# First shift's columns of blocks two to four on VectorE, conditions spread into the input tiles' buffer, parameters loaded with the third and fourth block

## The chip, the cores and the metric

The kernel runs on one core of a Trainium2 chip. The metric is the device time of one execution in microseconds, as the median of several runs; lower is better. The engines of the core are TensorE (PE, with its weight loads as PEld), VectorE (DVE), ScalarE (ACT), GpSimd (POOL) and SyncE (SP, which here only issues transfers). GpSimd issues transfers too, on a queue of its own.

## The reference, cut to what matters

One layer of a diffusion trunk: three tiles of 128 tokens (one prompt tile, two sample tiles) of width 2048, attention of three kinds, and a mixture of experts. Ahead of both halves stands a modulation whose vectors come from a condition; the prompt tile has the condition `c_ctx`, the two sample tiles have `c`:

```python
def modulate(h, shift, scale):
    return h * (1 + scale) + shift

def adaln(cond, w_mod, b_mod):
    m = jax.nn.silu(cond) @ w_mod + b_mod
    return jnp.split(m[:, None, :], 6, axis=-1)

sh1, sc1, g1, sh2, sc2, g2 = adaln(cond_ctx, lp["w_mod"], lp["b_mod"])
mix, ctx_t = context_mixer(modulate(rms_norm(xp, lp["g_attn"]), sh1, sc1), lp)
```

`w_mod` is 2048 x 12288 in fp32, so each of its six groups is 16 MB. The change is about the first two groups, the first shift (SH1) and the first scale (SC1), which are needed before any projection can start. All is fp32.

## The kernel before, in words

**Weights.** SyncE loads all weights in a fixed order of units of up to 1 MB into a ring of 12 slots (`units` in `plan`, the loop at line 776). Unit m waits until unit m - 12 is done with its slot (`frees`, lines 674 to 717). Two of the nine column chunks of the input projection, `ckv` (320 columns) and `cq0` (384 columns), are "early": they are computed while the modulation vectors are still being made. Their weights are cut into four pieces along the rows and go into two buffers of their own (`early_w`, lines 784 to 788); piece i waits until piece i - 2 has been used.

**The first blocks.** The 2048 columns of SC1 and SH1 are cut into four blocks of 512 columns (i = 0 to 3, called blocks one to four). A block has eight units, four of SC1 and then four of SH1, each with 512 rows of the weight; behind them come the two early weights of the block. On TensorE `first_unit` (line 842) multiplies a unit by the two conditions and a gain row (`csil`, three columns), four products side by side. When the four units of a group are in, VectorE adds the bias row (`first_copy`, L1626), TensorE turns the row into columns (`first_turn`, L859), and VectorE takes the columns out of the bank (`first_mod`, L1636, L1637, L1633). The outcome is `mod_t`: per row k of the transposed input one scale and one shift for each condition, with 128 features on the partitions. Then VectorE scales the transposed input in place (`hmod`, L1645), row by row, and TensorE multiplies the rows by the early weights (`early_part`, L883).

**The order on TensorE** is written out by hand (`next_units`, line 905, and the loop at line 912). A block of early projections has eight parts (four rows, two chunks each). After part 0 come units 0 and 1 of the *next* block, after part 1 units 2 and 3, then one unit after each of the parts 2 to 5; the scale row is turned after part 3 and the shift row after part 6. The first block's units stand before the loop, between the transposes of the input (`turn_xn`, L871). A block starts once both of its early weights have landed (line 879) and its first row is scaled (line 881).

```python
for n in ((0, 1), (2, 3), (4,), (5,), (6,), (7,), (), ())[part]:
    first_unit(i, n // 4, n % 4)
if part in (3, 6):
    first_turn(i, part // 6)
```

**GpSimd** loads the bias rows and the gain row at the start (lines 2143 to 2145), then works out the norms of the input (lines 2147 to 2150), then waits for turns: at the third (line 2151) it loads the rest of the constants, at the seventh (line 2153, the fourth block's scale) the gains and biases of all norms (lines 2154 to 2158) and the cached keys (lines 2159 to 2162). The norm of the first projection waits for these (line 1823).

**ScalarE** takes half of the transposed input out of its banks (line 1398) and then has nothing to do until the first projection is complete (L1431).

**After the blocks** the other projections, the attentions, the later four modulation groups, the output projection and the experts follow. The last modulation group is summed on VectorE (`g2_step`, L1800): a row of its weight, times the condition's value in that row, is added to a sum; two passes over 128 x 2048 per row.

Of the kernel before, what the change touches and what calls it, by code (L numbers as in the profile page):

```python
# [24 lines left out]
P = 128  # L25
D = 2048
# [48 lines left out]
FIRST_GROUPS = (SC1, SH1)  # L75
OUT_ORDER = [(0, 0), (0, 1), (0, 2), (1, 0), (1, 1), (1, 2), (2, 0), (2, 1), (3, 0), (3, 1), (2, 2), (3, 2)]
# [74 lines left out]
def plan():  # L151
# [27 lines left out]
    for i in range(4):  # L179
        units.extend(("first", g, i, m) for g in FIRST_GROUPS for m in range(4))  # L180
# [130 lines left out]
def by_units(w_mod, w_in, w_o):  # L311

    out = {}
    first = w_mod[0].reshape(P, 4, 4, 6, 4, 512)[:, :, :, list(FIRST_GROUPS)]
    out["w_first"] = first.transpose(3, 4, 1, 0, 2, 5).reshape(2, 4, 4, P, D)
# [7 lines left out]
def build(nc, ins, outs):  # L323
# [54 lines left out]
    with ExitStack() as ctx:  # L378
# [73 lines left out]
        junk_x, first_rows = r3_at(0, D), (r3_at(9728, D), r3_at(D, D))  # L452
# [108 lines left out]
        def acc_done(n):  # L561
# [43 lines left out]
        cols_in, brow_full, brow_ready, bias_full, bias_ready, wr_scaled = (sem(n) for n in (  # L605
            "cols_in", "brow_full", "brow_ready", "bias_full", "bias_ready", "wr_scaled"))
# [4 lines left out]
        ge_in, ge_out, re_in, re_out = sem("ge_in"), sem("ge_out"), sem("re_in"), sem("re_out")  # L611
# [22 lines left out]
        def unit_source(u, e=0):  # L634
# [5 lines left out]
            if kind == "first":  # L640
                _, g, i, m = u
                return ins["w_first"][FIRST_GROUPS.index(g), i, m].rearrange("p (q n) -> p q n", q=4), (4, 512)
# [32 lines left out]
        for i in range(4):  # L675
            for m in range(4):
                for c, g in enumerate(FIRST_GROUPS):
                    u = unit_no[("first", g, i, m)]
                    if m == 3:
                        frees[u] = (first_full, 2 * i + c + 1)  # L680
                    else:
                        slot_uses[ring_slot(u)] += 1
        uses = [0] * SLOTS
        for u in range(unit_no[("first", FIRST_GROUPS[1], 3, 3)] + 1):
# [87 lines left out]
        def _(sp):  # L772
# [3 lines left out]
            for m, u in enumerate(units):  # L776
# [5 lines left out]
                if u[0:2] == ("first", FIRST_GROUPS[1]) and u[3] == 3:  # L782
                    i = u[2]
# [53 lines left out]
        def _(pe):  # L837
# [4 lines left out]
            def first_unit(i, c, m):  # L842
# [4 lines left out]
                if m == 0:  # L847
                    if i:
                        pe.wait_ge(modt_ready, 2 * i + c - 1)
# [5 lines left out]
            def first_turn(i, c):  # L855

                pe.wait_ge(first_copied, 2 * i + c + 1)
# [3 lines left out]
                mm.then_inc(modt_full, 1)  # L861

# [70 lines left out]
            def tp_bank(s):  # L933
# [3 lines left out]
                else:  # L937
                    pe.wait_ge(modt_ready, 8)
# [40 lines left out]
            def spread_row():  # L979
# [5 lines left out]
                mm.then_inc(bias_full, 1)  # L985
# [389 lines left out]
        def _(act_e):  # L1375
# [24 lines left out]

            def cols_out(n):
# [171 lines left out]
            e.activation(g_s, g_s, ACT.Exp).then_inc(ge_out, 1)  # L1573
# [24 lines left out]
        def _(v):  # L1598
# [8 lines left out]
            v.memset(csil[:, :, 2:3], 0.0)  # L1607
            v.memset(first_ps[0][:, :], 0.0)
# [13 lines left out]
            def first_copy(i, c):  # L1622
                if i == 0 and c == 0:
                    v.wait_ge(first_rows_in, 3 * 16)
                v.wait_ge(first_full, 2 * i + c + 1)
# [3 lines left out]
            def first_mod(i, c):  # L1629
                v.wait_ge(modt_full, 2 * i + c + 1)  # L1630
# [10 lines left out]
            def hmod(i):  # L1641
                v.wait_ge(modt_ready, 2 * i + 2)
                for k in range(4 * i, 4 * i + 4):
# [3 lines left out]
                    last.then_inc(h_ready, 1)  # L1647

# [10 lines left out]
            v.wait_ge(xn_read_a, 6)  # L1659
            v.wait_ge(xn_read_v, 6)  # L1660
# [626 lines left out]
```

## Time and profile before

| What | Value |
| --- | --- |
| Median of 3 runs | 1689.63 us (1689.2 to 1691.83) |
| Profiled execution | 1689.92 us, of which the span is 1688.1 us |
| TensorE busy | 1587.0 us (94%) |
| VectorE, ScalarE, GpSimd busy | 690.1, 263.6, 106.1 us |
| Moved by the transfers | 581.94 MB, mean 345 GB/s |
| Chain that ended last | TensorE 67%, transfers 18%, VectorE 4% of the span |

The span is the profile's; the run's own time is 1.8 us longer. The window view gives the busy time of each engine in a stretch, the granted clock of TensorE (1.00 is 2.4 GHz, 0.50 is 1.2 GHz), the busy share of the transfer engines and their rate. In the timeline, instructions of one form that follow each other are merged into one row; a product in fp32 leaves two records. In the view of one line, "DMA to landing" is the time from the issue of a transfer to its landing.

### The profile page before, as it was taken

The page shows a single profiled execution, that of the slowest core. Times are in us where ns is not written, and L with a number is a line of the kernel's source. Part 1 is how long each engine was busy: PE and PEld are TensorE (multiplying, and loading weights), DVE is VectorE, ACT ScalarE, POOL GpSimd, SP SyncE. Part 2 cuts the span into 40 slices and gives each one's busy share as a digit, 9 for nine tenths or more (in the row PEclk, how much of TensorE's full clock was granted, in tenths as well). Part 3 has the DMA queues.
Part 4 walks back from the last instruction along what each step waited for, and adds up shares of the span by engine and source line. Part 5 has one row for each costly group of instructions (what it writes and reads, how often), then busy time and mean ns, then how long its engine had stood idle before and what let it go on. Part 6 is the DMA issues. An engine that isn't in the chain of part 4 may idle for free.

```text
span 1688.1 us, 18209 instructions
## 1 busy us (share of the span) xinstructions
PE 1587.0 (94%) x6671; PEld 654.3 (39%) x6716; DVE 690.1 (41%) x1361; ACT 263.6 (16%) x706; POOL 106.1 (6%) x192
## 2 busy tenths in 40 slices
PE   5999999999999999999999899899999899988998
PEld 2455555544434444443332332333233233233322
DVE  2113132113245893443444335444434434544444
ACT  2004221112133000011101101110110111011010
POOL 1022100100020100000000000000000000000000
PEclk8999999999999999999999999999999999999999
DMA  9993643535199765599999999999999999999995
GB/s 394 420 384 124 231 193 108 223 112 217 53 369 410 275 264 247 202 363 426 425 428 427 429 428 427 427 428 429 426 425 426 427 427 423 428 426 428 421 428 240
DMA packets 60526, 581.94 MB, mean 345 GB/s; under 512 B 9129, under 2 KB 10121, under 8 KB 16105
## 3 DMA queue, kind: packets, MB, share of 16 engines
q1 hardware_dynamic: 53120, 557.34, 79.8%
q0 software_dynamic: 6064, 23.22, 3.6%
q10 hardware_dynamic: 1296, 0.77, 0.2%
q8 instruction: 28, 0.46, 0.1%
q14 instruction: 18, 0.15, 0.0%
HBM read 584.06 MB, written 7.05 MB: 350 GB/s over the span
## 4 chain that ended last, share of the span: by engine, by line
PE 67%; DMA 18%; DVE 4%; issue 2%; ACT 1%; SPq 0%; POOL 0%; ACTq 0%
PE bank L1304 23%; DMA ring<-in_w 17%; PE bank L1052 13%; PE bank L1031 7%; PE bank L1214 7%; PE bank L1337 3%; DVE r L1800 2%; PE bank L926 2%; PE bank L1139 2%; PE bank L1263 2%; PE bank L1200 1%; PE bank L1114 1%; PE bank L1122 1%; PE bank L1319 1%; PE bank L1071 1%
## 5 line engine op out<-in xcount | busy, mean ns | idle before, releaser
L1304 PE MATMUL bank<-ring,r 128*64 128x512 f32 x1920 | 466.6, 616 | 45.1 <-DMA ring<-in_w 44.9
L1304 PEld LDWEIGHTS bank<-ring,r 128*64 128x64 f32 x1920 | 129.1, 139 | 300.6 <-issue 300.6
L1052 PE MATMUL bank<-ring,r 128*128 128x384 f32 (+1 forms) x672 | 240.7, 517 | 0.0
L2020 DVE TENSOR_TENSOR bank<-bank,r 128x512 f32<-128x512 f32 x180 | 126.0, 700 | 262.8 <-PE bank L1214 262.8
L1337 PE MATMUL bank<-ring,mod_row 128*64 128x512 f32 x896 | 195.6, 594 | 8.0 <-ACT mod_row L1553 7.9
L1031 PE MATMUL bank<-ring,r 128*128 128x512 f32 x384 | 170.0, 595 | 0.0
L1052 PEld LDWEIGHTS bank<-ring,r 128*128 128x128 f32 x672 | 126.3, 190 | 102.7 <-issue 43.2
L1214 PE MATMUL bank<-r 128*128 128x512 bf16 x495 | 137.7, 382 | 7.1 <-issue 7.0
L2022 DVE TENSOR_TENSOR r<-r,bank 128x512 f32<-128x512 f32 x180 | 123.8, 688 | 6.2
L1337 PEld LDWEIGHTS bank<-ring,mod_row 128*64 128x64 f32 x896 | 75.2, 137 | 118.7 <-issue 108.5
L1214 PEld LDWEIGHTS bank<-r 128*128 128x128 bf16 x540 | 38.0, 97 | 167.4 <-DVE r L2022 97.4
L1031 PEld LDWEIGHTS bank<-ring,r 128*128 128x128 f32 x384 | 71.2, 191 | 79.4 <-issue 79.3
L2043 DVE TENSOR_SCALAR gains<-bank,w_now 128x512 f32<-128x512 f32 x30 | 22.5, 751 | 175.0 <-PE bank L1337 162.0
L1800 DVE SCALAR_TENSOR_TENSOR r<-ring,csil,r 128x2048 f32<-128x2048 f32 x32 | 74.3, 2348 | 5.6 <-DMA r<-in_b_mod 5.0
L1828 DVE SCALAR_TENSOR_TENSOR r<-r,small,gains 128x128 f32<-128x128 f32 (+1 forms) x91 | 27.2, 343 | 120.9 <-POOL small L2138 115.8
L1876 DVE TENSOR_REDUCE small<-bank 128x1 f32<-128x384 f32 (+1 forms) x48 | 22.5, 468 | 129.7 <-PE bank L1114 77.3
L1431 ACT ACTIVATE r<-bank 128x128 f32<-128x128 f32 (+2 forms) x79 | 22.1, 289 | 324.6 <-PE bank L1052 215.8
L883 PE MATMUL bank<-r 128*128 128x320 f32 (+1 forms) x192 | 64.2, 481 | 1.2 <-DVE r L1645 1.2
L1542 ACT ACTIVATE r<-bank 128x512 f32<-128x512 f32 x30 | 17.8, 595 | 301.7 <-PE bank L1200 301.7
L1548 ACT ACTIVATE gain_row<-bank 128x512 f32<-128x512 f32 x16 | 9.6, 597 | 275.3 <-PE bank L1304 261.6
L2266 POOL COPY gat_now<-r 128x1 int32 x14 | 2.5, 182 | 747.9 <-PE bank L1200 747.9
L926 PE MATMUL bank<-ring,csil 128*2 128x512 f32 x384 | 47.4, 592 | 0.0
(283 smaller groups left out, 1237.8 us busy)
## 6 DMA issues: line engine op xcount, KB each, us to landing
ring<-in_w SPq DMA_DIRECT2D x180, 2048.0 KB, 17.4
ring<-in_w_mod SPq DMA_DIRECT2D x64, 1024.0 KB, 11.7
ring<-in_w_first SPq DMA_DIRECT2D x32, 1024.0 KB, 25.8
ring<-in_w SPq DMA_DIRECT2D x18, 1024.0 KB, 9.3
ring<-in_w_o SPq DMA_DIRECT2D x16, 1024.0 KB, 6.6
r<-mod_d POOLq DMA_DIRECT2D x8, 1024.0 KB, 8.4
ring<-in_w_aq SPq DMA_DIRECT2D x8, 768.0 KB, 11.3
ring<-in_w_bq SPq DMA_DIRECT2D x8, 768.0 KB, 12.9
```

The source lines that it names most:

```text
L883: mm = pe.matmul(early_bank[3 * c + t][:, 0:w], h_t[:, k, t * P:(t + 1) * P], early_w[c][i % 2][:, jj, :], start=(k == 0), stop=(k == KD - 1))
L926: mm = pe.matmul(mod_ps[32 * q:32 * q + 2, :], csil[:, k, 0:2], ring[:, ring_slot(m), q * 512:(q + 1) * 512], start=(k == 0), stop=(k == K ...
L1031: mm = pe.matmul(acc[acc_of(a)][:, :], qo[:, t, k, :], wu[:, j, :], start=(k == 0), stop=(k == KD - 1))
L1052: mm = pe.matmul(acc[acc_of(a)][:, 0:w], h_t[:, k, t * P:(t + 1) * P], wu[:, j, :], start=(k == 0), stop=(k == KD - 1))
L1139: mm = pe.matmul(out, v, prob_t[u % 2][:, i, :] if g == "C" else prob_ab[batch_of(u) % 2][:, i, :], start=(i == 0), stop=(i == len(tiles) ...
L1214: mm = pe.matmul(y_ps[k % 4][:, :], of_token[:, t * P:(t + 1) * P], y_part[:, n_part, c, :], start=(n_part == 0), stop=(n_part == 2))
L1263: mm = pe.matmul(ps[64 * c:64 * c + 64, :], xg_t[:, j, 64 * c:64 * c + 64], first_place(u)[:, j % 4 * 512:j % 4 * 512 + 512], start=(j == ...
L1304: mm = pe.matmul(ps[64 * c:64 * c + 64, :], xg_t[:, j, 64 * c:64 * c + 64], big_cut(slot_of(u), (8, 512))[:, j % 8, :], start=(j == 0), st ...
L1337: mm = pe.matmul(y_ps[c][64 * h:64 * h + 64, :], act_t[:, f, 64 * h:64 * h + 64], big_cut(slot_of(u), (2, D))[:, f % 2, c * 512:(c + 1) * ...
L1800: last = v.scalar_tensor_tensor(out=g2_sum[:, c, :], in0=ring[:, ring_slot(m), :], scalar=csil[:, k, c:c + 1], in1=g2_sum[:, c, :], op0=AL ...
L2020: v.tensor_tensor(ps[:, :], ps[:, :], g2b[:, min(t, 1), cols], ALU.mult).then_inc(strip_scaled, 1)
L2022: return v.tensor_tensor(x1[:, t, cols], x1[:, t, cols], ps[:, :], ALU.add)
```

## The change

Blocks two to four of SH1 no longer go through TensorE. Their 12 columns of `mod_t` (128 features each, k = 4 to 15) become units of a new kind, `("shift", k)`: the transposed weight, 128 output features on the partitions and 2048 inputs along the row, 1 MB each, in the place of the four SH1 units of the block. VectorE multiplies such a unit by a condition that is spread over all partitions, and sums along the row, one pass for each condition (`shift_columns`).

The conditions are spread at the start: GpSimd loads them as rows, TensorE multiplies them by a column of ones into banks (`spread_cond`, eight products, placed after the second and the third of the first block's shift units), and ScalarE takes them out with a Silu into the part of the input tiles' buffer that is free after the transposes (`cond_all`). TensorE waits for all eight before block one.

ScalarE scales the transposed input for k = 4 to 15; VectorE keeps k = 0 to 3. On TensorE one unit of the next block's scale stands after each of the parts 1 to 4 of a block, and its turn after part 5. GpSimd loads the gains and biases at the turn of the third block's scale, the cached keys at that of the fourth's. Two semaphores of the later stages are shared with the new steps, to stay within their number (not shown). The core of the diff:

```diff
     for i in range(4):
-        units.extend(("first", g, i, m) for g in FIRST_GROUPS for m in range(4))
+        units.extend(("first", SC1, i, m) for m in range(4))
+        units.extend(("shift", 4 * i + m) if i else ("first", SH1, i, m) for m in range(4))
...
+    out["w_shift"] = w_mod[0][:, SH1 * D + SHIFT_FROM * P:(SH1 + 1) * D].T.reshape(KD - SHIFT_FROM, P, D)
+    out["b_shift"] = b_mod[0][SH1 * D:(SH1 + 1) * D].reshape(KD, P).T
...
-        junk_x, first_rows = r3_at(0, D), (r3_at(9728, D), r3_at(D, D))
+        junk_x, first_rows = r3_at(0, D), (r3_at(9728, D), r3_at(D, 512))
+        ones_c, cond_rows, b_shift = r3_at(D + 512, P), r3_at(D + 640, 2, 512), r3_at(D + 1664, KD)
+        cond_all, junk_s = r2[:, 0:2 * D].rearrange("p (c n) -> p c n", c=2), r2[:, 2 * D:2 * D + D // 2].bitcast(BF16)
...
+                    if c and i:
+                        frees[unit_no[("shift", 4 * i + m)]] = (modt_ready, shift_count(4 * i + m))
+                        continue
...
+            def spread_cond(n0, n1):
+                for n in range(n0, n1):
+                    c, q = n // 4, n % 4
+                    mm = pe.matmul(spread_bank[n][:, :], ones_c[32 * q:32 * q + 1, :], cond_rows[32 * q:32 * q + 1, c, :],
+                                   start=True, stop=True)
+                mm.then_inc(spread_full, 1)
...
-            for m in range(4):
-                first_unit(0, 1, m)
+            first_unit(0, 1, 0)
+            first_unit(0, 1, 1)
+            pe.wait_ge(first_rows_in, 6 * 16)
+            pe.wait_ge(xn_read_a, 6)
+            pe.wait_ge(xn_read_v, 6)
+            spread_cond(0, 4)
+            first_unit(0, 1, 2)
+            pe.wait_ge(modt_ready, scale_count(0))
+            pe.wait_ge(cond_ready, 1)
+            spread_cond(4, 8)
+            first_unit(0, 1, 3)
             first_turn(0, 1)
+            pe.wait_ge(cond_ready, 8)
             def next_units(i, part):
-                for n in ((0, 1), (2, 3), (4,), (5,), (6,), (7,), (), ())[part]:
-                    first_unit(i, n // 4, n % 4)
-                if part in (3, 6):
-                    first_turn(i, part // 6)
+                if 1 <= part <= 4:
+                    first_unit(i, 0, part - 1)
+                elif part == 5:
+                    first_turn(i, 0)
...
+            for n in range(8):
+                c, q = n // 4, n % 4
+                ps = (xn_banks + (first_ps[0], xn_banks[0]))[n]
+                e.wait_ge(spread_full, 1 + c)
+                e.activation(cond_all[:, c, q * 512:(q + 1) * 512], ps[:, :], ACT.Silu).then_inc(cond_ready, 1)
+            for k in range(SHIFT_FROM, KD):
+                e.wait_ge(modt_ready, column_count(k))
+                for c, cols in enumerate((slice(0, P), slice(P, T))):
+                    last = e.activation(h_t[:, k, cols], h_t[:, k, cols], ACT.Identity, bias=mod_t[:, 1, k, c:c + 1],
+                                        scale=mod_t[:, 0, k, c:c + 1])
+                last.then_inc(h_ready, 1)
...
+            def shift_columns(k):
+                m = unit_no[("shift", k)]
+                v.wait_ge(*full_of(m))
+                if k == SHIFT_FROM:
+                    v.wait_ge(cond_ready, 8)
+                else:
+                    v.wait_ge(modt_ready, shift_count(k - 1))
+                w = ring[:, ring_slot(m), :]
+                for c in range(2):
+                    last = v.tensor_tensor_reduce(junk_s, w, cond_all[:, c, :], 1.0, b_shift[:, k:k + 1], ALU.mult, ALU.add,
+                                                  mod_t[:, 1, k, c:c + 1])
+                    if c == 0:
+                        after(last)
+                last.then_inc(modt_ready, 1)
...
-            hmod(0)
+            first_hmod()
             for i in range(1, 4):
-                for c in range(2):
-                    first_copy(i, c)
-                    first_mod(i, c)
-                hmod(i)
+                first_copy(i, 0)
+                shift_columns(4 * i)
+                first_mod(i, 0)
+                for k in range(4 * i + 1, 4 * i + 4):
+                    shift_columns(k)
...
+            g.dma_start(b_shift, ins["b_shift"]).then_inc(first_rows_in, 16)
+            g.dma_start(cond_rows[0:P:32, 0, :], ins["c_ctx"].rearrange("(q n) -> q n", q=4)).then_inc(first_rows_in, 16)
+            g.dma_start(cond_rows[0:P:32, 1, :], ins["c"][0].rearrange("(q n) -> q n", q=4)).then_inc(first_rows_in, 16)
...
-            g.wait_ge(modt_full, 7)
+            g.wait_ge(modt_full, first_count(2, 0))
             for name, dst in gain_of.items():
                 g.dma_start(dst, ins[name][0].partition_broadcast(P)).then_inc(gains_in, 16)
...
+            g.wait_ge(modt_full, first_count(3, 0))
             g.dma_start(cached["c"], ins["cache_c_kv"][0, 0]).then_inc(cache_k_in, 16)
...
-            g.wait_ge(modt_full, 8)
             load_row(LATER_GROUPS[0])
```

`first_count(2, 0)` is 4 and `first_count(3, 0)` is 5: with the shift turns of blocks two to four gone, these are the turns of the third and the fourth block's scale.

## Rows read from the trace of the kernel before

**Rows 1.** The page: TensorE and the transfers in 40 slices of the span.
```profile
PE   5999999999999999999999899899999899988998
...
DMA  9993643535199765599999999999999999999995
```

**Rows 2.** Windows of 20 us: stretch, length, busy us per engine, PEclk, DMA, GB/s.
```profile
80.00:100.00 20.00, 20.00 (x105) 8.93 (x104) 3.96 (x11) 0.00 (x0) 0.00 (x0) 1.00 1.01 420
...
140.00:160.00 20.00, 18.73 (x64) 10.41 (x63) 5.99 (x26) 8.99 (x45) 5.71 (x12) 1.00 0.01 5
```

**Rows 3.** Timeline, 37 to 130 us: start, length, engine, line, operation, tiles, records.
```profile
38.16 3.54 PE L883 MATMUL bank<-r 128*128 128x320 f32 x6 [1.16 <-DVE r L1645]
...
62.82 3.80 PE L883 MATMUL bank<-r 128*128 128x384 f32 x12
...
70.94 0.11 PEld L851 LDWEIGHTS bank<-ring,csil 128*3 128x3 f32 x4 [0.32 <-DMA ring<-in_w_first]
...
72.33 1.88 PE L883 MATMUL bank<-r 128*128 128x320 f32 x6
...
74.15 1.04 PE L851 MATMUL bank<-ring,csil 128*3 128x512 f32 x8
...
87.53 3.80 PE L883 MATMUL bank<-r 128*128 128x384 f32 x12
...
112.24 16.38 PE L883 MATMUL bank<-r 128*128 128x384 f32 x54
```

**Rows 4.** Early weights (L788), one issue each: blocks three and four, then landing.
```profile
L788 SPq DMA_DIRECT2D r<-in_w_cq x1: 327/327/327, 65.0 to 65.0; - x1
...
DMA to landing us min/median/max: 19.1/19.1/19.1
...
L788 SPq DMA_DIRECT2D r<-in_w_cq x1: 327/327/327, 89.7 to 89.7; - x1
...
DMA to landing us min/median/max: 17.7/17.7/17.7
```

**Rows 5.** VectorE passes over 128x2048, two sources and one: ns min/median/max, first and last start.
```profile
L1800 DVE SCALAR_TENSOR_TENSOR r<-ring,csil,r x32: 2341/2351/2352, 557.4 to 639.3; 128x2048 f32<-128x2048 f32 x32
...
L1613 DVE TENSOR_SCALAR r<-r,small x3: 1276/1285/1286, 9.3 to 18.3; 128x2048 f32<-128x2048 f32 x3
```

**Rows 6.** Ring loads (L781) of block four: issues 68.9 to 73.2 and 75.4 to 77.6.
```profile
L781 SPq DMA_DIRECT2D ring<-in_w_first x3: 2126/2133/2138, 68.9 to 73.2; - x3
...
DMA to landing us min/median/max: 25.2/25.5/25.8
...
L781 SPq DMA_DIRECT2D ring<-in_w_first x2: 433/1284/2134, 75.4 to 77.6; - x2
...
DMA to landing us min/median/max: 26.1/26.3/26.4
```

**Rows 7.** ScalarE's groups to 150 us: busy us, mean ns, then idle before and releasers.
```profile
L1398 ACT ACTIVATE r<-bank 128x512 f32<-128x512 f32 x6 | 3.4, 592 | 1.9 <-PE bank L871 1.9
...
L1431 ACT ACTIVATE r<-bank 128x128 f32<-128x128 f32 (+2 forms) x15 | 4.6, 316 | 115.2 <-PE bank L883 103.4 <-PE bank L1052 9.6 <-PE bank L1071 2.0
```

**Rows 8.** GpSimd's timeline; the bracket is the idle time before, with its releaser.
```profile
8.38 0.19 POOL L2149 TENSOR_SCALAR small<-small 128x1 f32<-128x1 f32 x1 [2.06 <-ACT r L1387]
...
104.29 0.55 POOL L2155 DMA_DIRECT2D gains<-in_a_qn  x1 [48.79 <-PE bank L859]
```

**Rows 9.** Ring loads (L781) that follow block four's early weights.
```profile
L781 SPq DMA_DIRECT2D ring<-in_w_cq x4: 430/449/2124, 90.1 to 91.6; - x4
...
DMA to landing us min/median/max: 20.4/25.6/29.6
```

**Rows 10.** Queues, 104 to 125 us: packets, MB, share of the 16 engines.
```profile
q0 software_dynamic: 608, 1.05, 23.2%
```

**Rows 11.** Windows of 1 us, columns as in rows 2: TensorE's clock falls and returns.
```profile
31.00:32.00 1.00, 0.00 (x1) 0.00 (x0) 0.00 (x0) 0.00 (x0) 0.00 (x0) 0.93 1.01 410
32.00:33.00 1.00, 0.57 (x4) 0.11 (x8) 0.00 (x0) 0.00 (x0) 0.00 (x0) 0.50 1.05 431
...
42.00:43.00 1.00, 1.00 (x12) 0.19 (x8) 0.00 (x0) 0.00 (x0) 0.00 (x0) 0.95 1.04 434
```

More of the change, by code:

```diff
@@ L75, with first_count, shift_count, scale_count @@
 FIRST_GROUPS = (SC1, SH1)
+SHIFT_FROM = 4
+def first_count(i, c):
+    return i + 2 if i else c + 1
+def shift_count(k):
+    i, j = k // 4, k % 4
+    return 2 + 5 * (i - 1) + (j + 2 if j else 1)
+def scale_count(i):
+    return 2 + 5 * (i - 1) + 2 if i else 1
+def column_count(k):
+    return max(shift_count(k), scale_count(k // 4)) if k >= SHIFT_FROM else 2
 OUT_ORDER = [(0, 0), (0, 1), (0, 2), (1, 0), (1, 1), (1, 2), (2, 0), (2, 1), (3, 0), (3, 1), (2, 2), (3, 2)]
@@ L308, with by_units @@
         ("state_c_kv", (1, 1, P, KV_RANK)), ("state_c_krope", (1, 1, P, ROPE))]
-def by_units(w_mod, w_in, w_o):
+def by_units(w_mod, b_mod, w_in, w_o):
     out = {}
-    first = w_mod[0].reshape(P, 4, 4, 6, 4, 512)[:, :, :, list(FIRST_GROUPS)]
-    out["w_first"] = first.transpose(3, 4, 1, 0, 2, 5).reshape(2, 4, 4, P, D)
+    first = w_mod[0].reshape(P, 4, 4, 6, 4, 512)
+    out["w_scale"] = first[:, :, :, SC1].transpose(3, 1, 0, 2, 4).reshape(4, 4, P, D)
+    out["w_shift0"] = first[:, :, :, SH1, 0].transpose(1, 0, 2, 3).reshape(4, P, D)
+    out["w_shift"] = w_mod[0][:, SH1 * D + SHIFT_FROM * P:(SH1 + 1) * D].T.reshape(KD - SHIFT_FROM, P, D)
+    out["b_shift"] = b_mod[0][SH1 * D:(SH1 + 1) * D].reshape(KD, P).T
     rows = w_in[0].reshape(4, 4, P, -1)
@@ L641, in unit_source @@
                 _, g, i, m = u
[L642 removed]
+                w = ins["w_scale"][i, m] if g == SC1 else ins["w_shift0"][m]
+                return w.rearrange("p (q n) -> p q n", q=4), (4, 512)
+            if kind == "shift":
+                return ins["w_shift"][u[1] - SHIFT_FROM], (D,)
             if kind == "in":
@@ L683, in build @@
         uses = [0] * SLOTS
-        for u in range(unit_no[("first", FIRST_GROUPS[1], 3, 3)] + 1):
+        for u in range(unit_no[("shift", KD - 1)] + 1):
             if u not in frees:
@@ L781, in _ @@
                 sp.dma_start(cut(slot, shape), src).then_inc(slot_full[slot], 16)
-                if u[0:2] == ("first", FIRST_GROUPS[1]) and u[3] == 3:
-                    i = u[2]
+                if u == ("first", SH1, 0, 3) or u[0] == "shift" and u[1] % 4 == 3:
+                    i = u[1] // 4 if u[0] == "shift" else 0
                     for c, name in enumerate(EARLY):
@@ L1639, in first_mod, with first_hmod @@
                                            op0=ALU.add, op1=ALU.mult).then_inc(modt_ready, 1)
-            def hmod(i):
-                v.wait_ge(modt_ready, 2 * i + 2)
-                for k in range(4 * i, 4 * i + 4):
+            def first_hmod():
+                v.wait_ge(xn_read_a, 6)
+                v.wait_ge(xn_read_v, 6)
+                v.wait_ge(modt_ready, column_count(0))
+                for k in range(SHIFT_FROM):
                     for c, cols in enumerate((slice(0, P), slice(P, T))):
@@ L2277 @@
     arrays = {f"in_{n}": np.ascontiguousarray(inputs[n]) for n in IN_NAMES if n not in ("w_in", "w_o")}
-    for n, a in by_units(inputs["w_mod"], inputs["w_in"], inputs["w_o"]).items():
+    for n, a in by_units(inputs["w_mod"], inputs["b_mod"], inputs["w_in"], inputs["w_o"]).items():
         arrays[f"in_{n}"] = np.ascontiguousarray(a)
```

37 lines of the change are left out of this document (20 added, 17 removed).

## The prediction

> **What bounds the kernel now.** I read the page first, then the stretch before the first projections, then the transfers there. Over the whole span TensorE has nearly no idle slice, so what shortens or lengthens its work early moves the end by as much [rows 1]. In the first 100 us the DMA engines are full as well, at 420 GB/s; only from 140 us, with every ring slot filled, do they rest [rows 2]. So this stage has two limits side by side, and the change touches both.
>
> The timeline shows TensorE's side. The merged rows that begin with the last piece of a block start at 62.82, 87.53 and 112.24 us: 24.7 us a block [rows 3]. Between the pieces of the early projections (1.88 us with 320 columns) stand the units of the first shift and scale (1.04 us) [rows 3]. The last block has no units: 54 records in 16.38 us, 48 of them its own, so 14.3 us for a block of projections alone; block four starts at 114.3 and ends at 128.6 us.
>
> The transfers' side: a block needs eight units and two early weights, 9.83 MB, or 23.4 us at 420 GB/s. The last early weight of block three was issued at 65.03 and landed 19.1 us later, at 84.1; that of block four at 89.75 + 17.7 = 107.45 us [rows 4]. The distance is 23.4 us, as by the bytes. TensorE began block four only 6.9 us after its last weight was there. **That lead is all that faster engines can win here**: no byte of the weights goes away.
>
> **The change, part by part.**
>
> *Units taken off TensorE.* A block loses four units and one turn of ten such pieces; (24.7 - 14.3) / 10 = 1.04 us each, so 5.2 us a block and 15.6 us over three. TensorE's block becomes 19.5 us, shorter than the transfers' 23.4. From block two on TensorE then waits for data, and of the 15.6 us at most 6.9 can be kept.
>
> *Columns on VectorE.* Twelve columns, two passes each over 128x2048 of two fp32 sources in SBUF. The trace has no such pass. Nearest is the two-source pass of the last modulation group, which reads the ring too: 2.35 us; below lies the one-source pass of that size, 1.28 us, above it twice the two-source pass, 4.7 us, should the sum cost a second reading [rows 5]. I take 2.35, same shape and number of sources. A column is 4.7 us, a block 18.8 plus a copy and a modulation of about 1.1: 19.9, within 23.4. The order on VectorE matters: a block's first column stands behind the copy of its scale row, which waits for TensorE's fourth unit. In block two that copy ends near 54 us (block one starts at 38.16, four pieces and four units in, the first at the low clock), and the twelve columns could be through at 54 + 24 x 2.35 + 3 = 113 us. Block four's columns also wait for their data: today the fourth scale unit lands at 68.9 + 25.2 = 94.1, the next unit near 96.9, the last at 77.6 + 26.4 = 104.0 us [rows 6]. With the delay below, the first column starts near 101 and the fourth ends near 120 us; ScalarE's scaling adds 0.7, and TensorE wants it at about 123. So the columns hide, with 2 to 3 us to spare.
>
> The Trainium skill, Vector Engine (DVE) Microarchitecture Reference, section on points that are easy to get wrong, says that an STT-shaped instruction with two SBUF sources that are not bf16 runs at half rate, for want of a port for the accumulator. The existing pass has that shape and those sources and shows no half rate (2.35 us beside 1.28 with one source); with an accumulator no run here shows it. By that rule of the Trainium skill a column would be 9.4 us, my estimate, twice the measured pass.
>
> *Scaling on ScalarE.* Twelve pairs, by the 316 ns mean of its early activations some 0.7 us a pair [rows 7]; it has sat idle for over 100 us here, so they cost the first 0.7 us of a column's delay, counted above. VectorE sheds as much.
>
> *The spread.* Eight one-row products and eight Silu of some 592 ns (the copies of that size [rows 7]) go in before block one, and TensorE waits for all eight. Four such products take 1.04 us if they share the array like a unit's four [rows 3], and 3.5 us if one by one (0.30 us a record by the last row of [rows 3], scaled to 512 columns, two records each); double at the low clock. Most fits into the waits for units up to 32 us; the delay of block one is 0 to 7 us. It costs nothing, because block two would be over near 80 us and must wait for the weights of block three at 84 and later. If that wait were gone, it would cost those 0 to 7.
>
> *GpSimd's queue.* Three more loads stand ahead of its first scaling, at 0.55 us an issue [rows 8], 1.65 in all; it idles 2.06 us there [rows 8]. Nothing.
>
> *SyncE.* As many transfers in the same order; but a ring slot of a shift column is now freed by VectorE. The unit that lands at 94.1 reuses the slot of the fourth column of block two, free near 74 us: 20 us ahead, and other transfers are queued before it. Nothing, until a pass exceeds some 3 us.
>
> *The parameters.* Now they are asked for at 104.29 us [rows 8], when the last early weights are about to land, and what they push back is the next weights. Those four units, issued up to 91.6, should follow at 107.45 + 7.5 (3.15 MB) = 114.95 and landed at 91.6 + 29.6 = 121.2: 6.25 us late [rows 9]. Beside them the software queue took 23.2% of the engines' time over 21 us, 4.9 us, for 1.05 MB [rows 10]. After the change the gains and biases (597 KB) go out at the third block's scale turn, near 76 us (its last unit landed at 70.9 [rows 3]), and the cached keys (416 KB) at the fourth's, near 103: **ahead of the early weights on which block four waits.** By bytes the first lot is 59%, 3.7 us, all in front; of the other 2.55 us I take half; the new small loads 0.2. Bounds: 0.2, if the packets slip behind, and 6.5. I take 5.2, since two thirds are asked for 30 us before the deadline.
>
> *The clock.* TensorE fell to half its clock at 32 us, after it had waited for units, and was back at 42 us, four us into block one; its first piece there took 3.54 us instead of 1.88 [rows 3, 11]. That row prices a cold start at 1.7 us for the piece and about 1.9 for the block. With the change TensorE stands still for some 6 us before block four (block three over near 107, weights at 112.7). Bounds 0 and 1.9; I take 1.0, since no wait of this length after a busy stretch is in the trace.
>
> **Sum.** Block four starts at 107.45 + 5.2 = 112.65 instead of 114.3, and ends at 112.65 + 14.3 + 1.0 = 127.95 instead of 128.6: 0.7 us earlier. Behind it the first projection has its weights 6 us before it needs them, and the work up to the expert stage follows TensorE, so the end moves by as much. The profiled execution took 1689.92 us (span 1688.1), 0.3 above the median: 1689.2 for it, 1688.9 us as a median. Bounds of the forecast: a delay of 6.5 and a cold start, 114.0 + 14.3 + 1.9 = 130.2 (+1.6), and a delay of 3.5 and none, 111 + 14.3 = 125.3 (-3.3); that is 1686.3 to 1691.2.
>
> **Rivals.**
>
> *The parameters don't hold up the weights* (faster). If GpSimd issues them slowly or the engines favour the hardware queue, block four starts at 107.65 and ends at 122.0, or 123.9 with a cold start: 4.7 to 6.6 us saved, 1683.0 to 1684.9. For it: issues on GpSimd will stand beside two-source VectorE passes, which this trace has not; slowed issues would land later, perhaps too late to matter. Against it: today's 6.25 us push, on the same queues. (The Trainium skill, GPSIMD Engine Reference, section Specifications, says that GpSimd shares its SBUF interfaces with VectorE and contends with its instructions that have two SBUF inputs; no run here shows by how much.)
>
> *The pass with a sum is slow* (slower). The columns set the end when 54 + 24x + 3 + 4.3 exceeds 128.6, from x = 2.8 us a pass. At 4.7 the chain ends at 174 us, 45 later: 1735. Against it: the existing pass. For it: an instruction the trace doesn't show. It is what the rule quoted above from the Trainium skill's Vector Engine (DVE) Microarchitecture Reference would do; the trace does not bear it out without an accumulator, and is silent with one.
>
> *The change doesn't do what it says*: no, the units and the turn are gone from TensorE's list.
>
> **Chances.** Forecast, with the clock and the parameters within their bounds, 0.63; parameters out of the way 0.24; slow pass 0.10; another delay before block one than I can place 0.03. A measurement tells about 0.2%, 3.4 us: below 1686.2 counts as faster, above 1693.0 as slower. That gives 0.24 faster, 0.63 within, 0.13 slower. The range takes in the forecast and most of the first rival, 1683.5 to 1692.0; the likeliest case alone is 1686.3 to 1691.2.
>
> **What would show it.** Right: TensorE waits for early weights before blocks three and four; block four starts within 2 us of 112.7 and runs 14 to 16; the parameter loads land before its weights; the passes take 2.35 us and VectorE rests before each block's first. Wrong: block four starts by 109 (parameters cheap), passes over 2.8 us with TensorE waiting for ScalarE's h, or a start of block one so late that block two ends after 88.

## The result, and the profile of the changed kernel

The changed kernel takes 1693.72 us (median of 10 runs, 1691.29 to 1696.04), beside 1689.3 us for the kernel before in the same comparison (10 runs). The ratio is 1.0022, 95% interval 1.0014 to 1.003: slower by 0.2%, 3.7 us by the ratio and 4.4 as the difference of the medians. The forecast, 0.7 us the other way, and its range up to 1692.0 both missed.

The profiled execution is the fastest of the ten, 1691.29 us with a span of 1689.5 (before 1688.1). TensorE's busy time fell by 8.2 us (1578.8 against 1587.0): units and turns alone fell by 15.9 us (12.6 and 3.3, forecast 15.6), but the spread added 2.3 and the blocks' products, in part at the low clock, 3.2. VectorE's rose to 736.0. So the work was moved as meant, and the time went into waits. TensorE's timeline from the end of block two on:

```profile
75.73 3.80 PE L929 MATMUL bank<-r 128*128 128x320 f32 x12
90.14 6.66 PE L929 MATMUL bank<-r 128*128 128x320 f32 x12 [10.62 <-DMA r<-in_w_cq]
...
109.22 3.80 PE L929 MATMUL bank<-r 128*128 128x320 f32 x12
114.17 7.57 PE L929 MATMUL bank<-r 128*128 128x320 f32 x24 [1.15 <-DMA r<-in_w_cq]
122.82 3.82 PE L929 MATMUL bank<-r 128*128 128x320 f32 x12 [1.08 <-ACT r L1468]
127.72 3.82 PE L929 MATMUL bank<-r 128*128 128x320 f32 x12 [1.08 <-ACT r L1468]
...
131.75 4.68 PE L1108 MATMUL bank<-ring,r 128*128 128x384 f32 x14
```

Block three waits 10.62 us for its early weights and starts at 90.14, no earlier than in the kernel before, where it follows on the piece that begins at 87.53 [rows 3]: all that TensorE won in block two is lost here. Block four starts at 114.17, as before, but then its rows wait for ScalarE (L1468), and the next projection (L1108) starts at 131.75, 2.9 us later than before (L1052 there):

```profile
128.85 1.46 PE L1052 MATMUL bank<-ring,r 128*128 128x384 f32 x4
```

The transfers show why block three waits. The `cq0` weights of block three and of block four were issued at 59.19 and 88.71 us; they landed 30.9 and 25.4 us later, at 90.1 and 114.1:

```profile
L824 SPq DMA_DIRECT2D r<-in_w_cq x1: 327/327/327, 59.2 to 59.2; - x1
...
DMA to landing us min/median/max: 30.9/30.9/30.9
...
L824 SPq DMA_DIRECT2D r<-in_w_cq x1: 2749/2749/2749, 88.7 to 88.7; - x1
...
DMA to landing us min/median/max: 25.4/25.4/25.4
```

Between them GpSimd issued the gains, from 76.17 to 81.57 us. Windows of the same trace (stretch, length, busy us of PE, PEld, DVE, ACT, POOL, then granted clock, DMA share, GB/s):

```profile
72.00:78.00 6.00, 6.00 (x30) 3.68 (x28) 5.73 (x6) 0.99 (x2) 1.83 (x4) 1.00 1.02 426
78.00:82.00 4.00, 1.53 (x5) 0.57 (x3) 3.93 (x7) 0.98 (x2) 3.57 (x7) 1.00 1.18 330
82.00:86.00 4.00, 0.00 (x0) 0.00 (x0) 3.82 (x5) 0.98 (x2) 0.00 (x0) 0.53 0.80 134
86.00:90.00 4.00, 0.00 (x0) 0.00 (x0) 3.85 (x3) 0.98 (x2) 0.00 (x0) 0.50 1.00 342
90.00:96.00 6.00, 5.86 (x11) 3.54 (x12) 3.12 (x4) 0.98 (x2) 0.00 (x0) 0.51 1.01 409
```

From 82 to 86 us the transfer engines are 80% busy and move 134 GB/s, a third of the usual rate. Both queues are slow then (packets, MB, share of the 16 engines): the gains take 37.2% for 0.14 MB, and the weights beside them 42.9% for 0.40 MB.

```profile
q1 hardware_dynamic: 74, 0.40, 42.9%
q0 software_dynamic: 64, 0.14, 37.2%
```

TensorE stands still meanwhile, its clock falls to 0.50 (1.2 GHz, called cold below), and the first 12 records of block three take 6.66 us instead of 3.80.

On VectorE the new work is as cheap as hoped. The pass with its sum, the read of the accumulator and ScalarE's scaling:

```profile
L1733 DVE CUSTOM_DVE_ANT_0 r<-ring,r x24: 2341/2351/2352, 53.3 to 124.3; 128x2048 bf16<-128x2048 f32 x24
L1733 DVE DVE_READ_ACCUMULATOR2_ANT mod_t<- x24: 80/82/84, 55.5 to 126.6; 128x1 f32 x24
...
L1468 ACT ACTIVATE r<-r,mod_t x24: 492/539/587, 58.4 to 127.1; 128x128 f32<-128x128 f32 x12, 128x256 f32<-128x256 f32 x12
```

### The profile page after: what moved, and what is told of

Read it like the earlier page. It is cut to its first block, busy times and chain, and to the rows that moved or that the text cites. A ratio compares the mean times of both kernels' runs of the same rounds, so it can differ in the third digit from the quotient of the medians.

```text
span 1689.5 us, 18067 instructions
## 1 busy us (share of the span) xinstructions
PE 1578.8 (93%) x6567; PEld 653.2 (39%) x6612; DVE 736.0 (44%) x1380; ACT 279.6 (17%) x738; POOL 106.4 (6%) x195
## 4 chain that ended last, share of the span: by engine, by line
PE 68%; DMA 16%; DVE 4%; issue 2%; ACT 1%; SPq 0%; POOL 0%; ACTq 0%
PE bank L1360 24%; DMA ring<-in_w 15%; PE bank L1108 13%; PE bank L1270 7%; PE bank L1087 7%; PE bank L1393 3%; DVE r L1889 2%; PE bank L982 2%; PE bank L1195 2%; PE bank L1319 2%; PE bank L1256 1%; PE bank L1408 1%; PE bank L1342 1%; PE bank L1170 1%; PE bank L1178 1%
## 5 line engine op out<-in xcount | busy, mean ns | idle before, releaser
L1108 PE MATMUL bank<-ring,r 128*128 128x384 f32 (+1 forms) x672 | 240.7, 517 | 0.0
L1108 PEld LDWEIGHTS bank<-ring,r 128*128 128x128 f32 x672 | 126.2, 190 | 102.8 <-issue 43.2
L1733 DVE CUSTOM_DVE_ANT_0 r<-ring,r 128x2048 bf16<-128x2048 f32 x24 | 56.4, 2350 | 1.3
L929 PEld LDWEIGHTS bank<-r 128*128 128x128 f32 x192 | 37.4, 204 | 46.8 <-issue 14.5
```

Of the source, the lines that this page charges most:

```text
L929: mm = pe.matmul(early_bank[3 * c + t][:, 0:w], h_t[:, k, t * P:(t + 1) * P], early_w[c][i % 2][:, jj, :], start=(k == 0), stop=(k == KD - 1))
L1108: mm = pe.matmul(acc[acc_of(a)][:, 0:w], h_t[:, k, t * P:(t + 1) * P], wu[:, j, :], start=(k == 0), stop=(k == KD - 1))
L1733: last = v.tensor_tensor_reduce(junk_s, w, cond_all[:, c, :], 1.0, b_shift[:, k:k + 1], ALU.mult, ALU.add, mod_t[:, 1, k, c:c + 1])
```

## Experiments

Four terms were in question: the place of the parameter loads, what makes them dear, the columns' chain, and the cold clock. Medians and ratios are over several runs; rows and starts come from one profiled execution of each kernel, and two traces of the changed kernel differ by 1.0 us at the next projection (part 5).

### 1. Where the parameters are asked for

**The fourth block's turn** (e1): `- g.wait_ge(modt_full, first_count(2, 0))`, `+ g.wait_ge(modt_full, first_count(3, 0))` ahead of the gains, all else as changed.

> The changed kernel with the gains and biases asked for at the fourth block's scale turn, as before the change. Theory P (the parameter loads stall the weights, TensorE waits and comes back at half clock, and the scale copy and the columns behind it come late): block three starts near 84.5 us instead of 90.1, without a long wait; the same push, some 6 us, now falls on the weights of block four, which starts near 113 and ends at 128 to 130 instead of 131.5. 1690 to 1692 us. Theory C (the columns on VectorE set the end by themselves): block four still ends near 131, 1693.7 us.

**After block four's early weights** (e5): `- g.wait_ge(modt_full, first_count(2, 0))`, `+ g.wait_ge(early_in[1], 2 * 32)`.

> The changed kernel with all parameter loads behind the landing of the last early weight. Theory P: no push on any early weight; block three starts near 84.5, block four near 108, its columns are ready at about 102 to 118, it ends at 122 to 124; 1682.5 to 1685 us. Theory C: the end of block four moves by less than 2 us, 1692 to 1694 us. If the norm behind the first projections then waits for the gains, up to 4 us of this come back.

**The kernel before, with the gains moved alone** (e3): `- g.wait_ge(modt_full, 7)`, `+ g.wait_ge(modt_full, 5)` ahead of the gains; the cached keys stay at 7.

> The kernel before with one part of the change alone: gains and biases asked for at the third block's scale turn, the cached keys left at the fourth's. Theory P: the weights of block three land near 90 and those of block four near 113.5 instead of 84.1 and 107.45; TensorE, which starts these blocks at 89.6 and 114.3 there, loses at most 1 us: 1689 to 1690.5 us. If the loads pushed by only 3.7 us, as forecast, there is no change at all: 1689.3 us.

| Kernel | Median us (runs) | Ratio to before (95%) | Next projection starts (one trace) |
| --- | --- | --- | --- |
| before, for e1, e5 and e3 | 1690.09 (27) | | 128.85 |
| changed | 1693.72 (10) | 1.0022 (1.0014 to 1.003) | 131.75 |
| e1, gains at the fourth | 1688.62 (11) | 0.999 (0.9981 to 0.9999) | 127.71 |
| e5, all after early weights | 1686.58 (11) | 0.9982 (0.9973 to 0.9991) | 125.88 |
| e3, before with gains at the third | 1697.99 (5) | 1.0042 (1.0029 to 1.0056) | 133.05 |

The changed kernel's ratio is to its own comparison. The later its gains are asked for (76.2, 100.9 and 107.8 us), the shorter its time. In e1 block three is on time, and block four waits instead and runs at the low clock:

```profile
84.22 3.82 PE L929 MATMUL bank<-r 128*128 128x320 f32 x12 [1.79 <-DMA r<-in_w_cq]
...
110.83 16.66 PE L929 MATMUL bank<-r 128*128 128x320 f32 x48 [6.57 <-DMA r<-in_w_cq]
```

Its median came below the 1690 to 1692 us that were expected, since block four started at 110.83 and not near 113. e3 is the clearest: without a column on VectorE, the moved gains alone make the kernel before 7.9 us slower by the medians, 4.2 of them by the next projection (of the rest the part on what stays open has some). Both outcomes that were expected of e3, at most 1 us lost or nothing, failed. Its timeline shows the cost in a place that the prediction had not looked at, the scale units of block four (L851), not the early weights:

```profile
94.92 1.04 PE L851 MATMUL bank<-ring,csil 128*3 128x512 f32 x8 [2.51 <-DMA ring<-in_w_first]
...
100.27 1.04 PE L851 MATMUL bank<-ring,csil 128*3 128x512 f32 x8 [1.21 <-DMA ring<-in_w_first]
```

The lead of 6.9 us belonged to the early weights. The units had next to none: in the kernel before one already waits 0.32 us at 70.94 [rows 3].

With the loads out of the way (e5), block three starts 6 us earlier than in the changed kernel and block four at 107.59. Then the columns set the end, which is why the median misses the expected 1682.5 to 1685:

```profile
84.19 6.75 PE L929 MATMUL bank<-r 128*128 128x320 f32 x12 [3.60 <-DMA r<-in_w_cq]
...
107.59 3.82 PE L929 MATMUL bank<-r 128*128 128x320 f32 x12 [0.44 <-DMA r<-in_w_cq]
112.05 3.82 PE L929 MATMUL bank<-r 128*128 128x320 f32 x12 [0.65 <-ACT r L1468]
116.95 3.82 PE L929 MATMUL bank<-r 128*128 128x320 f32 x12 [1.08 <-ACT r L1468]
121.85 3.82 PE L929 MATMUL bank<-r 128*128 128x320 f32 x12 [1.08 <-ACT r L1468]
```

### 2. What makes these loads dear

The gains come by ten loads that give the same few numbers to all 128 partitions. e8 and e10 lay them out for 128 partitions in memory beforehand, and leave them at the third block's turn, where the change put them. e8 fetches them by one load, e10 by ten of the old widths:

```diff
-            for name, dst in gain_of.items():
-                g.dma_start(dst, ins[name][0].partition_broadcast(P)).then_inc(gains_in, 16)
...
+            g.dma_start(gains[:, 0:off[0]], ins["gains"]).then_inc(gains_in, 16)
```
```diff
+            at = 0
+            for dst in (*gain_of.values(), sink, r_bias[:, 0:GROUPS], r_bias[:, GROUPS:]):
+                g.dma_start(dst, ins["gains"][:, at:at + dst.shape[-1]]).then_inc(gains_in, 16)
+                at += dst.shape[-1]
```

> The changed kernel, with the gains and biases still loaded at the third block's scale turn, but laid out for all 128 partitions in memory beforehand and fetched by one load of 0.61 MB in place of ten broadcast loads. Theory A (the ten loads cost TensorE's weights about 5.9 us because their packets are small and many, 0.61 MB holding the engines for 4.5 us against 1.25 us for the 0.44 MB of cached keys): with one load the share of the software queue falls to about 1.5 to 2 us, block three's weights land at 85.5 to 87 instead of 90.1, next projection at 127 to 129, median 1688 to 1690.5. Rival B (bytes set the price, or any load of the software queue stops the hardware queue): block three's weights land at 89 to 91 as in the changed kernel and the median is 1693 to 1694.

> As e8, but the laid-out gains and biases are fetched by ten loads of the same widths as the broadcast loads, at the same turn: same bytes, same packet sizes, same issues, only that each partition reads its own row. Theory A1 (number and size of the packets set the price): as in the changed kernel, block three's weights land at 89 to 91, median 1693 to 1694. Theory A2 (128 partitions reading the same few bytes of memory is what is slow): the weights land at 85.5 to 87 as in e8, median 1688 to 1690.5.

The software queue over 74 to 96 us: packets, MB, share of the 16 engines. First the changed kernel:

```profile
q0 software_dynamic: 368, 0.61, 20.5%
```

then e8,

```profile
q0 software_dynamic: 144, 0.61, 7.1%
```

and e10:

```profile
q0 software_dynamic: 368, 0.61, 7.9%
```

Same bytes in all three, and in e10 the same 368 packets; yet the broadcast takes 20.5% of 22 us, 4.5 us, against 1.6 and 1.7. So what is dear is the broadcast, neither the bytes nor the number of packets: in the changed kernel 128 partitions read the same few bytes. (The laid-out copy is also one array in memory where the gains were ten; no run separates the two.) Block three started at 85.69 and 86.09, the next projection at 127.53 and 127.80. The medians came to 1689.96 and 1689.12 (11 runs each; ratios 0.9994, 0.9986 to 1.0003, and 0.9996, 0.9987 to 1.0005): 3.8 to 4.6 us off the changed kernel's 1693.72, as expected of the broadcast and not of the packets. The Trainium skill, Perfetto Trace Analysis, section DMA Optimizations, says that transfers under 2 KB carry a significant overhead each; here the step from ten loads (368 packets) to one (144) is worth 0.8% of 22 us, 0.2 us. The broadcast is worth 2.8.

The same in the kernel before (e12: e3 with e10's ten loads):

> The kernel before with the gains and biases at the third block's scale turn, as in e3, but laid out for all partitions and fetched by ten loads, as in e10. Theory (e3 lost 4.2 us at the next projection because ten broadcast loads slow the engines for some 6 us; laid out they take 1.7): the scale units of block four come at most 1.7 us late, next projection at 128.9 to 130, median 1689.5 to 1692. Rival (any load there hits the scale units): next projection at 132 or later, median 1696 or more.

1690.89 us, ratio 1.0006 (0.9997 to 1.0015), next projection at 129.22: of e3's 7.9 us nearly all is gone, with the loads in the same place.

### 3. The order of the columns

e2 puts the first column ahead of the scale row's copy (changed kernel otherwise):

```diff
-                first_copy(i, 0)
                 shift_columns(4 * i)
+                first_copy(i, 0)
```

> The changed kernel with the first column of a block ahead of the copy of the scale row on VectorE, all else as it is. Theory P: the first column of block four lands only near 105 us, because the stream is late, so VectorE starts it 2 us earlier than the 107.1 of the changed kernel; block four ends 1 to 2 us earlier, near 130: 1692 to 1693 us. Theory C: VectorE has rested 13 us before that column, and putting it first takes most of a column, 4.9 us, out of the chain: 1689 us.

1691.88 us, ratio 1.0009 (1.0 to 1.0018), next projection at 129.28. It gains 2.5 us on the changed kernel there, and no row of block four waits for ScalarE. But this is not the order alone: the turn that sends the gains comes later too, they are asked for from 80.55 us instead of 76.17, and block three starts near 86.5, after the first 12 records of the row at 80.11, without a wait for weights. And the copy now waits behind a column, and TensorE's turn waits for the copy, 3.32 and 4.09 us:

```profile
78.82 1.43 PE L895 MATMUL bank<-cst,mod_row 128*128 128x3 f32 x8 [3.32 <-DVE mod_row L1698]
80.11 10.34 PE L929 MATMUL bank<-r 128*128 128x320 f32 x24
...
80.55 0.56 POOL L2248 DMA_DIRECT2D gains<-in_a_qn  x1 [23.08 <-PE bank L895]
...
107.00 1.87 PE L895 MATMUL bank<-cst,mod_row 128*128 128x3 f32 x8 [4.09 <-DVE mod_row L1698]
```

e7 starts from e5 and loads a block's four shift units first; the four columns precede the copy, and the scale units stand after the parts 6 and 7:

```diff
+            units.extend(shift + scale if i else scale + shift)
...
-                first_copy(i, 0)
-                shift_columns(4 * i)
-                first_mod(i, 0)
-                for k in range(4 * i + 1, 4 * i + 4):
+                for k in range(4 * i, 4 * i + 4):
                     shift_columns(k)
+                first_copy(i, 0)
+                first_mod(i, 0)
```

> The changed kernel with the parameters asked for only after block four's early weights (as in e5), and in each of blocks two to four the shift units loaded ahead of the scale units, the four columns ahead of the scale's copy on VectorE, and the scale units after the parts 6 and 7 on TensorE. Theory (in e5 the columns set the end of block four: TensorE waits 0.65, 1.08 and 1.08 us for ScalarE's h there, because the first column stands behind the scale row's copy): columns of block four run 83 to 103 us, the rows are scaled at 0.98 us each from about 106, TensorE starts block four at about 108, waits for no row and takes 14.3 us plus 0 to 3 of cold clock: next projection at 122 to 125 (e5 125.9, before 128.9), median 1683 to 1686. Rival (the copy and the turn after the last scale unit now stand on the path): block four starts after 110 and the next projection stays at 125.5 or later, median 1686.5 or more.

```profile
105.96 0.69 DVE L1699 TENSOR_TENSOR mod_row<-bank,r 128x512 f32<-128x512 f32 x1
...
109.32 16.13 PE L930 MATMUL bank<-r 128*128 128x320 f32 x48 [1.56 <-ACT r L1469]
```

No row of block four waits any more, but the block waits for the copy behind the fourth column and for what follows it, 105.96 to 109.32, and runs cold at first (granted clock 0.63 from 110 to 114 us), 16.13 instead of 14.3. The next projection starts at 125.67, 0.2 us before e5's; the median is 1688.23 (ratio 0.9992, 0.9983 to 1.0002), 1.7 us worse than e5's. The expectation fails: one wait took the place of the other.

### 4. The cold clock

e9 adds products of no use to e5, ahead of block three:

```diff
             for i in range(4):
+                if i == 2:
+                    for n in range(5):
+                        pe.matmul(first_ps[1][:, 0:T], ident, h_t[:, 0, :], start=True, stop=True)
                 for part in range(8):
```

> e5 with five products of no use (384 columns of h_t into the first shift's bank, some 3.2 us) on TensorE ahead of block three, in the time in which it waits for weights. Theory (the low clock at block three comes from TensorE's standing still): the first 12 records of block three take 3.8 to 4.2 us instead of 6.75 with the clock at 1.00 through 84 to 90; block four's scale units, copy and first column come up to 2.9 us earlier, and the next projection at 123 to 124.5 instead of 125.9: median 1684 to 1685.5. Rival (the clock falls for another reason, or the chain behind block four's columns is set by its units' landing): the 12 records stay near 6.75, or they shorten and the next projection still starts at 125.5 to 126, median 1686.5.

```profile
80.55 3.39 PE L971 MATMUL bank<-r,cst 128*128 128x384 f32 x10
84.41 3.82 PE L929 MATMUL bank<-r 128*128 128x320 f32 x12 [0.47 <-DMA r<-in_w_cq]
...
107.74 15.93 PE L929 MATMUL bank<-r 128*128 128x320 f32 x48 [3.30 <-DMA r<-in_w_cq]
124.71 0.41 PE L1148 MATMUL bank<-cst,r 128*128 128x128 f32 x2 [1.04 <-DVE r L1920]
124.95 1.46 PE L1111 MATMUL bank<-ring,r 128*128 128x384 f32 x4
```

The price is shown: 3.82 us for the 12 records instead of 6.75, so standing still cost 2.9 us there. It hardly pays: TensorE waits 3.30 us before block four instead, which then ends sooner but not soon enough for the norms (L1920). The next projection starts 0.9 us earlier than in e5, short of the 123 to 124.5 that was expected, and the median is the same, 1686.6 (9 runs, 0.9982, 0.9971 to 0.9992).

e11 tried to take the rest: e9, warm products before block four as well, the gains by one load, and two shift units before the four scale units and two behind them, with the columns in that order.

```diff
+            units.extend(shift[:2] + scale + shift[2:] if i else scale + shift)
```

> e9 (parameters after block four's early weights, warm products on TensorE ahead of block three) with three more edits: warm products ahead of block four as well, the gains by one laid-out load, and in blocks two to four two shift units ahead of the four scale units, two behind (columns, copy and scale units follow). Theory (what is left in e9 is the columns chain of block four, 103.5 to 118 us, and a cold clock of 1.6 us): block four starts at 107.5 to 108.5, waits for no row of ScalarE's, and ends 14.3 to 14.6 us later: next projection at 122 to 123 (e9 123.9, before 128.9), median 1683.5 to 1686. Rival (the first row of block four now waits for the scale, which is made one column later): block four starts at 109 or later and the median stays at 1686.5 or above.

1690.61 us, ratio 1.0003 (0.9994 to 1.0012), next projection at 128.48. The scale is made later, so block three started only at 89.99 and block four at 113.83, each after a wait for ScalarE (0.61 us); the rival was right. What was gained is the clock: block four took 14.44 us.

### 5. A second trace of the changed kernel

> The changed kernel once more, for a second trace: the one at hand is of its fastest execution (1691.29 us, median 1693.7). Theory (beyond the first 130 us the difference between executions is TensorE's clock, which in some of them falls at two short waits near 380 and 724 us, as in the traces of e1, e2 and e3): the trace shows the next projection at 131.5 to 132 again, and a time above 1693 goes with a granted clock under 1.00 at 376 to 392 or 720 to 736. Rival (the first stage itself differs from run to run): the next projection starts 1.5 us or more away from 131.75.

1692.7 us; the next projection started at 132.77, 1.0 us later than in the first trace. Block three waited less (it started at 88.41), block four more:

```profile
88.41 6.44 PE L929 MATMUL bank<-r 128*128 128x320 f32 x12 [7.62 <-DMA r<-in_w_cq]
...
115.19 17.35 PE L929 MATMUL bank<-r 128*128 128x320 f32 x48 [4.12 <-DMA r<-in_w_cq]
```

In this execution the early weights and a cold clock set block four, in the first one the rows did. The end of the stage is late either way, by 2.9 and 3.9 us. The next projection lies outside the theory's 131.5 to 132 and within the rival's 1.5 us, so neither is borne out; the clock was at 1.00 at 376 to 392 and at 720 to 736 us, and the run's time was below 1693.

## Why the prediction was wrong

**The failed step: the price and the place of the parameters.** It priced the gains by their share of the bytes, 59% of a push of 6.25 us, so 3.7. They hold the engines for 4.5 us by the queue's share, and the weights beside them are slowed too: block three's landed at 90.1 against 84.2 in e5, 5.9 us later (4.2 by the start in the second trace). A share by bytes was wrong because broadcast and plain loads of equal size differ by 2.6 times here. The cached keys took 5.2% of 24 us in the changed kernel, 1.25 us, for 0.44 MB; if they took as much before, 3.6 of the 4.9 us of [rows 10] were the gains', 74% and not 59%.

**And they hit more than block four.** The step let the push act on block four's early weights alone, behind a lead of 6.9 us. But they are asked for at 76 us, and the first transfer that TensorE waited for was block three's, at 84. Everything in between slid with it: TensorE stood still for 10.62 us, started cold (2.9 us, where the prediction had put 1.0, and before block four), and so made the scale row of block four late. Its copy came at 106.51 us; with the loads later (e5) it came at 100.64, and there the prediction's "near 101" for the first column holds. The changed kernel, then e5:

```profile
106.51 0.69 DVE L1698 TENSOR_TENSOR mod_row<-bank,r 128x512 f32<-128x512 f32 x1 [13.35 <-PE bank L887]
```
```profile
100.64 0.69 DVE L1698 TENSOR_TENSOR mod_row<-bank,r 128x512 f32<-128x512 f32 x1 [6.42 <-PE bank L887]
```

**"So the columns hide, with 2 to 3 us to spare"** failed in the first trace for that reason, and for two small sizes: a column came every 4.9 us instead of 4.7 (58.23 to 63.13), and ScalarE's pair took 0.98 us and not 0.7. The mean of [rows 7] mixes shapes, but that is not the cause. With the same two shapes the earlier activations, out of a bank, add up to 0.66 us; the scaling works within `r` with factors from `mod_t`, and which of these makes it slower no run separates. Before, then changed:

```profile
L1431 ACT ACTIVATE r<-bank 128x128 f32<-128x128 f32 x8 | 2.1, 273 | 2.0 <-PE bank L1071 2.0
...
L1431 ACT ACTIVATE r<-bank 128x256 f32<-128x256 f32 x3 | 1.2, 384 | 103.6 <-PE bank L883 103.4
```
```profile
L1468 ACT ACTIVATE r<-r,mod_t 128x256 f32<-128x256 f32 x12 | 7.0, 585 | 0.0
L1468 ACT ACTIVATE r<-r,mod_t 128x128 f32<-128x128 f32 x12 | 5.9, 493 | 81.4 <-DVE mod_t L1709 46.8 <-DVE mod_t L1733 34.6
```

In numbers: the forecast put the end of the block 0.65 us earlier, so the next projection at 128.2 instead of 128.85. It came at 131.75, 3.55 after the forecast. Block four's start, forecast at 112.65, was 114.17 (1.5). From there to the next projection it was 17.6 us, 3.0 more than before (128.85 less 114.3), by the waits for rows. The cold start put there did not come (less 1.0). In the second trace the start was 115.19 (2.5), and the same 3.0 us were lost to the cold clock. That block four started within the 2 us that the prediction allowed thus speaks for the limit by the transfers, not for its price of the parameters.

**Right:** the units off TensorE and the limit set by the transfers; the pass at 2.35 us, so that the slow-pass rival fell; the spread, which does not show at block one (it started at 37.06 and 38.33 in the two traces, and in eight more with the spread between 36.48 and 38.60, but for e1's 40.53; before at 38.16); the loads ahead of GpSimd's norms.

**The slower rival** took its price from a rule. The Trainium skill, Vector Engine (DVE) Microarchitecture Reference, section on points that are easy to get wrong, says that the form with two SBUF sources that are not bf16 halves the throughput. Read as twice the measured two-source pass, as the prediction read it, the row of L1733 (2351 ns with the sum) decides against it. But "shows no half rate" misread the row: 2.35 us is 1.8 times the 1.28 of one source [rows 5]. If the half is counted from there, the measured passes agree with it, with the sum and without.

**The faster rival** was no fiction: e5 is what it described, parameters that hold nothing up, and it beats both kernels (the one before by 0.2%). But it brought 3.0 us at the next projection instead of 4.7 to 6.6, since the columns chain, which the rival left out, ends the block at 125.7. Issues on GpSimd beside the two-source passes took 0.55 us as before, so the contention named for this rival does not show in them:

```profile
76.17 0.56 POOL L2248 DMA_DIRECT2D gains<-in_a_qn  x1 [19.73 <-PE bank L895]
```

**What stays open.** The medians differ by 4.4 us, the two traces of the changed kernel by 2.9 and 3.9 at the next projection; the last stage of the first trace gave 1.2 back, so its span is only 1.4 longer. In the traces of e1, e2 and e3 the clock falls once more near 380 and near 724 us, and in e3 these stages take 1.7 and 2.4 us longer than before, about half of the 7.9. Neither trace of the changed kernel has these falls, and the mean clocks listed with its runs do not order its times (0.986 at 1691.29, 1694.05 and 1694.24 us). In e1 they do: 0.987 to 0.989 in the five runs up to 1687.39, 0.982 to 0.985 in the five from 1690.31 on. What makes the changed kernel's other executions slower than its first trace stays open.

## What to carry to other kernels

Price a moved transfer by the engines' time in the trace, not by its bytes, and follow it to the first consumer behind it in the queue, not to the one that you have in mind; that consumer's lead is what it may cost. Small parameters that are broadcast from one row to all partitions were dear here beside a saturated stream: lay them out in memory, or ask for them once the last transfer with a deadline has landed. A lead belongs to one transfer; the next in the same stream may have none.

## What the runs showed of the hardware that was not expected

- A broadcast of 0.61 MB from ten short rows to 128 partitions slowed the whole stream to 134 GB/s for 4 us, with the engines 80% busy, and the weights of the other queue with it; over 74 to 96 us the mean was 335 GB/s, against 419 and 406 with the same bytes from 128 rows (e8, e10).
- The two-source pass with a sum runs as fast as without (2351 ns for 128x2048 fp32 sources, the result in bf16), and the read of the sum costs 82 ns.
- ScalarE's activation with a factor and an addend per partition took 493 and 585 ns within `r`, against 273 and 384 ns out of a bank without them, for the same shapes.
- TensorE's granted clock fell to 0.50 (1.2 GHz) around a wait of 3.60 us before block three (e5, 86 to 90 us: 6.75 us for 12 records) and around one of 6.57 us before block four (e1, 110 to 114 us: 16.66 us for 48 records instead of 14.3). It stayed at 1.00 where products of no use filled the wait (e9, 78 to 90 us).
